# Clearing matmuls on an idle PSUM bank behind the square sums of each norm, in a three-block transformer kernel

## The reference, cut to what matters

```python
def rmsnorm(x, g):
    xf = x.astype(jnp.float32)
    y = xf * lax.rsqrt(jnp.mean(xf * xf, axis=-1, keepdims=True) + NORM_EPS)
    return (y * g.astype(jnp.float32)).astype(x.dtype)

# first block
    h = modulate(rms_norm(x, norm_g[l, 0]), shift[:, 0], scale[:, 0])
    x = x + 0.5 * gate[:, 0, None, :] * swiglu(h, ffn1_w_in[l], ffn1_w_out[l])
    h = modulate(rms_norm(x, norm_g[l, 1]), shift[:, 1], scale[:, 1])
    x = x + gate[:, 1, None, :] * token_mixer(h, ...)
    h = modulate(rms_norm(x, norm_g[l, 2]), shift[:, 2], scale[:, 2])
    x = x + 0.5 * gate[:, 2, None, :] * swiglu(h, ffn2_w_in[l], ffn2_w_out[l])
    return rms_norm(x, final_g)

# second block, for each of two layers
    h = rmsnorm(x, norm1_g[l]) * (1.0 + sc1) + sh1
    x = x + g1 * (merged @ w_out[l])          # attention and a short convolution
    h = rmsnorm(x, norm2_g[l]) * (1.0 + sc2) + sh2
    x = x + g2 * peer(h, w_query[l], sub_keys[l], expert_u[l], expert_v[l])
```

## Time and profile before

| | before |
|---|---|
| median of 3 runs | 3389.08 us (3388.97 to 3389.96) |
| profiled execution | 3391.32 us |
| its span, first to last instruction | 3389.6 us |
| mean granted TensorE clock | 0.935 |
| TensorE busy | 3020.5 us, 89% |
| VectorE busy | 2484.9 us, 73% |
| ScalarE busy | 1358.3 us, 40% |
| GpSimd busy | 750.7 us, 22% |
| DMA, mean over the span | 162 GB/s |

### The profile page before, as it was taken

How to read it: one execution, slowest core, us unless ns; L and a number is a source line. 1 busy time by engine, 2 the same in 40 slices (tenths; PEclk the granted TensorE clock), 3 DMA queues, 4 the chain that set the end, 5 groups by cost and what they waited for, 6 DMA issues and landing times. The chain is left out here.

```text
span 3389.6 us, 62057 instructions
## 1 busy us (share of the span) xinstructions
PE 3020.5 (89%) x22464; PEld 2756.0 (81%) x22464; DVE 2484.9 (73%) x3349; ACT 1358.3 (40%) x1958; POOL 750.7 (22%) x588
## 2 busy tenths in 40 slices
PE   3998988889989778999998889998799999988898
PEld 2998976779979578989987668796799899866687
DVE  6777734357778566998999986644449889899865
ACT  2434532234344334544333335543345443333354
POOL 1011002101101000025765530000000256655300
PEclk7999986889989689999999999997899999999999
DMA  7784520048858345544444445552245444444454
GB/s 270 270 278 139 185 100 1 1 147 276 278 199 316 103 153 176 174 159 144 153 137 148 137 143 192 166 171 78 100 148 174 156 149 149 136 146 139 143 192 143
DMA packets 149585, 547.98 MB, mean 162 GB/s; under 512 B 16608, under 2 KB 16736, under 8 KB 149088
## 3 DMA queue, kind: packets, MB, share of 16 engines
q1 hardware_dynamic: 124704, 454.29, 39.8%
q0 software_dynamic: 24336, 89.14, 7.8%
q10 hardware_dynamic: 432, 2.97, 0.2%
HBM read 545.29 MB, written 1.05 MB: 161 GB/s over the span
## 5 line engine op out<-in xcount | busy, mean ns | idle before, releaser
L728 DVE TENSOR_TENSOR w_lo<-ring,w_hi 128x1024 fp32r<-128x1024 f32 x864 | 1140.4, 1321 | 542.8 <-ACT w_hi L390 539.9
L390 ACT ACTIVATE w_hi<-ring 128x1024 fp32r<-128x1024 f32 x864 | 910.8, 1054 | 1105.7 <-PE st L1447 915.6
L1443 PE MATMUL st<-h_hi,w_hi 128*128 128x256 f32 x4064 | 1038.7, 292 | 43.1 <-DVE h_lo L757 27.0
L1444 PE MATMUL st<-h_lo,w_hi 128*128 128x256 f32 x4064 | 1016.6, 287 | 0.0
L1443 PEld LDWEIGHTS st<-h_hi,w_hi 128*128 128x128 f32 x4064 | 793.7, 195 | 62.8 <-issue 38.6
L1444 PEld LDWEIGHTS st<-h_lo,w_hi 128*128 128x128 f32 x4064 | 796.2, 196 | 1.0
L1417 POOL TENSOR_TENSOR extra<-extra 128x512 bf16<-128x512 bf16 x384 | 565.7, 1499 | 429.5 <-DVE extra L1237 429.5
L1447 PE MATMUL st<-h_hi,w_lo 128*128 128x256 f32 x4064 | 581.9, 287 | 23.1 <-DVE w_lo L728 22.8
L1447 PEld LDWEIGHTS st<-h_hi,w_lo 128*128 128x128 f32 x4064 | 532.7, 195 | 29.5 <-DVE w_lo L728 29.3
L1237 DVE TENSOR_TENSOR extra<-extra,k 128x512 bf16<-128x512 f32 (+1 forms) x256 | 334.1, 1305 | 5.3 <-PE st L1811 2.8
L1837 PE MATMUL acc<-w_hi,act_hi 128*128 128x512 f32 x1024 | 325.4, 399 | 4.9 <-DVE act_lo L1253 4.9
(11 more groups left out here) (254 smaller groups left out, 3060.4 us busy)
## 6 DMA issues: line engine op xcount, KB each, us to landing
ring<-weights SPq DMA_DIRECT2D x864, 512.0 KB, 3.3
arena<-ada_weights POOLq DMA_DIRECT2D x168, 512.0 KB, 5.1
arena<-const ACTq DMA_DIRECT2D x1, 2112.0 KB, 8.7
x_t<-params SPq DMA_DIRECT2D x1, 1024.0 KB, 8.3
out<-arena POOLq DMA_DIRECT2D x1, 1024.0 KB, 4.2
k<-const ACTq DMA_DIRECT2D x1, 473.0 KB, 4.6
arena<-smallw ACTq DMA_DIRECT2D x1, 320.0 KB, 10.4
par<-params SPq DMA_DIRECT2D x1, 198.5 KB, 4.4
```

The lines of the kernel that those rows point to most:

```text
L390: nc_a.activation(w_hi[:, u % 2, :], ring[:, u % RING, :], ACT.Copy).then_inc(hi_ready, 1)
L728: v.tensor_tensor(w_lo[:, u % 2, :], ring[:, u % RING, :], w_hi[:, u % 2, :], ALU.subtract)\
L1443: mm(dst(t), w, hi_t(t), start=start, stop=False, skip_group_check=True)
L1444: mm(dst(t), w, lo_t(t), start=False, stop=False, skip_group_check=True)
```

## The change

`spin(bank, n)` issues n matmuls of one row of zeros by 512 columns, each of which clears a bank. Three places call it, always with bank 3 of `acc`: `squares` behind its increment of `sumsq`, 18 times; `product`, where `fresh` is given, once ahead of the wait for each of the tiles 1 to 7; and the code behind the transposes of the experts' part, 6 times ahead of `squares`.

```diff
+            def spin(bank, n):
+
+
+                for _ in range(n):
+                    mm(bank, zrow[0:1, :], zrow[0:1, :].unsqueeze(1).to_broadcast([1, 4, P]), start=True, stop=True,
+                       skip_group_check=True)
+
             def product(u, dst, hi_t, lo_t, i=None, per=0, first=False, last=False, shared=False, fresh=None):
...
                     if fresh is not None:
+                        if t > 0:
+                            spin(acc[:, 3, :], 1)
                         eng.wait_ge(sem("norm_lo"), DT * fresh + t + 1)
...
                     ins = mm(st[:, 3, 0:T], ones, nh[:, t, :], start=t == 0, stop=t == DT - 1)
                 ins.then_inc(sem("sumsq"), 1)
+                spin(acc[:, 3, :], 18)
...
                     ins.then_inc(sem("y_back"), 1)
+                spin(acc[:, 3, :], 6)
                 squares(6 + 2 * l)
                 stage(eng, ST[f"peer_d{l}"])
```

## The result

| | before | changed kernel |
|---|---|---|
| median | 3389.52 us (3388.97 to 3391.7, 4 runs) | 3456.64 us (3452.22 to 3458.32, 4 runs) |
| profiled execution, span | 3389.6 us | 3453.9 us |
| mean granted TensorE clock | 0.935 | 0.927 |

The ratio is 1.0195 (95% interval 1.0177 to 1.0212). The kernel became slower by 67 us, where 25 were forecast, and its time lies outside the range (3404 to 3436).

A forecast was written before the change was run, and what follows sets the result against it. The prediction took TensorE, busy for 89% of the span, to bound the kernel. Its terms, 30.3 + 2.1 - 6.0 - 1.4 = 25.0 us on the median of 3389.1, gave 3414.1 us, with a range of 3404 to 3436.

The forecast's parts named there:

- first term: At nine norms, the 18 matmuls ahead of the barrier hold TensorE's drain, delaying the reciprocal 3.37 us each: 30.3 us.
- second term: Six matmuls ahead of the square sums at two norms behind the experts move ScalarE's root by 1.06 us: 2.1 us.
- third term: Matmuls between tiles in seven first units shorten the half-clock time: -6.0 us, half of the 11.9 ceiling.
- (a): Clearing matmuls do nothing for the clock, and a 1.1 us lag stays in seven units: 3432 us, chance 0.20.
- (c): The 18 don't hold the barrier, because TensorE's drain lets it pass: 3376.5 us, faster, chance 0.04.
- fourth term: Fifth norm's square sums, at half clock before, gain from the fourth norm's clearing matmuls: -1.4 us, bounds 0 and 2.8.
- (b): The clock is full in every first unit and in the fifth norm's sums: 3407 us, chance 0.12.

The follow-up runs named there:

- full_rows: Changed kernel with every added matmul using 128 rows of ones and constants instead of one row of zeros; 3407.6 us, ratio 1.0049.
- behind_barrier: Changed kernel with each group of 18 clearing matmuls moved behind the barrier that follows the square sums; 3433.9 us, ratio 1.0116.
- only_between: Changed kernel with only the 49 one-row matmuls between the first unit's tiles, without the 18 and the six; 3416.7 us, ratio 1.0076.

## Why the prediction was wrong

The direction was right, and so was the mechanism of the first term. The second is about right in the trace and not clear of noise by itself. The third had the wrong sign.

**The first term** (9 x 3.37 = 30.3 us). The reciprocals start 4.04 us behind the end of the sums where they started 0.61 behind, at five norms, so 3.43 each; at the seventh and ninth 3.2. At the fourth and sixth it is 5.2 and 4.8, for the clock falls under the 18 (rival (a) had this, at 1.0 us and three norms; here it is 1.8 and 1.4 us at two). The fourth norm of the changed kernel:

```profile
987.19 5.80 PE L1438 MATMUL acc<-zrow 1*128 1x512 bf16 x18
...
993.05 1.75 DVE L753 RECIPROCAL extra<-extra 128x256 f32<-128x256 f32 x1 [8.96 <-PEq L319]
```

Together 33.6 us in the profiled execution; by itself the edit measured 31.7. That the drain holds the barrier is shown by the releaser PEq, and rival (c) is out.

**The second term** (2.1 us). At the seventh norm the sums start 1.93 us behind the start of the last four transposes instead of 0.44, and the root 1.38 us later, not 1.06:

```profile
2231.52 0.60 PE L1874 MATMUL acc<-k,arena 128*128 128x128 f32 x4
...
2232.05 1.46 PE L1438 MATMUL acc<-zrow 1*128 1x512 bf16 x6
...
2233.45 3.72 PE L1464 MATMUL st<-arena,k 128*128 128x256 f32 x16
```

The 0.2 us over the six lie at the two changes of rows. The size is about right, 2.8 us in the trace and 1.9 by itself, an interval that holds zero.

**The third term** (-6.0 us) is the step that failed. It said: "with a clearing matmul between any two tiles TensorE has no pause in the first unit, at half clock 0.42 + 2 x 0.21 = 0.85 us a tile", and the eighth tile 1.1 us late. It took 1.26 us a tile and 3.9 us in all (12.40 against 8.50). The price of 0.42 had been read from four clearing matmuls that follow one another, and used where each stands between 128-row products. There it delays the weight load of its own and that of the product behind it. So the first unit ends 3.9 us later, and TensorE pauses in it at every tile, though its modelled ends show 8.60 us busy of 8.60. The second half of the step failed too: one-row matmuls between the tiles were to let the clock rise earlier, and it rises later. By the fourth unit 24.35 - 19.61 = 4.74 us are lost, 3.9 of them already at the eighth tile; 7 x 4.74 = 33.2 us, where -6.0 stood. With 128 rows the term has the sign that was meant: 18.80 - 19.61 = -0.81 us a unit in full_rows, 7 x 0.81 = -5.7 us. That this is near -6.0 is luck, since -6.0 was half of a ceiling and not worked out.

**The fourth term** (-1.4 us). The fifth norm's sums took 5.46 us instead of 6.42: -1.0 us.

33.6 + 2.8 + 33.2 - 1.0 = 68.6 us; the spans differ by 64.3. The square sums of the second and the eighth norm were 1.7 and 1.1 us shorter (3.72 against 5.41 us, 5.41 against 6.54). The 1.5 us left over are a balance of larger ones: between the seventh and the eighth norm 2.5 us more were lost than these terms give, between the sixth and the seventh 2.4 less. Neither is traced.

**The rivals.** (a), 0.20, was nearer: it had the one-row matmuls not holding the clock, shown by behind_barrier and by the fourth norm above. But it too had 0.42 us for each in the first unit, and so 3432. (b) is out, for every first unit ran at half clock. Its argument was half right: at the sixth norm the clock fell within the wait, but at the second it was still at 1.00 through the 3.6 us without work and fell behind the first product, in the kernel before. The Trainium skill ("TensorE: Matmul & The Clock Gate", section "Step-by-step: what each phase is for") says that TensorE pulls a weight load ahead of running matmuls where row groups don't conflict or where it goes to the background buffer. The trace agrees for 128 rows next to 128 rows (0.00 us between the matmul's start and the next load's, at 297.23); between 64 rows or fewer and 128 the load isn't pulled ahead (0.53 us), and no run shows which of the two conditions fails there. That the overlap has conditions, and that no row showed a 1*128 matmul between 128*128 ones, should have put the price in doubt.

## What to carry to other kernels

Matmuls that are to keep TensorE's clock up belong behind the barrier that starts the wait, not ahead of it, and must have the rows of the work around them: 128 rows of zeros held the clock in this kernel, one row did not, and between the tiles 64 rows did no better than one. Price an added instruction by a row in which its neighbours are those it will have; between 128-row products a one-row matmul of 64 columns took 0.89 - 0.42 = 0.47 us at half clock, where its 64 columns at the pace of 0.42 us for 512 come to 0.05. And where an engine's ends are modelled, look at the distance of starts: "8.60 busy of 8.60" hid a pause at each tile.

## What the runs showed of the hardware that was not expected

- A matmul of 64, 32 or 1 rows next to 128-row ones delays weight loads on both sides. At half clock its start is 0.35 us behind that of a 256-column product (0.22 for 128 rows), and the load behind it starts 0.53 us after a 512-column matmul (0.00 for 128 rows); 0.16 us after one of 64 columns.
- Zeros on both sides, with 128 rows, count for the clock: it stayed at 1.00 through the 18 and 3.5 us of wait behind them, and fell 6.0 to 9.4 us behind the square sums. One row of zeros doesn't: the clock fell 2.1 to 5.3 us behind the sums, at the fourth norm under the 18 themselves (at 989 us). One row of ones costs the same by the median (3459.1 us).
- With one-row matmuls between the tiles of the first unit the clock stayed at half for 10.2 to 13.7 us at a norm (only_between), and for 13.7 to 20.5 with the 18 ahead of them too; in the kernel before for 6.8 to 10.2. Why it was still at 0.50 through 5 us of gapless products (315 to 320 us) stays open.
- At the same pace of 0.88 to 0.89 us a tile at half clock, the clock stayed at half for 3.4 to 6.8 us with 128 rows between the tiles and for 10.2 to 13.7 with one row of 64 columns.
